# Expert weights of a two-layer mixture-of-experts kernel: one 2 MB transfer per block in place of two of 1 MB, issued once the whole buffer has been read

## What is computed

```python
def grouped_moe(x, router_w, router_bias, w_gate, w_up, w_down):
    ...                       # choose 2 of 16 experts per token: gates, [256, 16]
    def step(acc, ew):
        g_e, wg_e, wu_e, wd_e = ew          # 1024x512, 1024x512, 512x1024
        h = jax.nn.silu(x2 @ wg_e) * (x2 @ wu_e)
        return acc + (h @ wd_e) * g_e[:, None].astype(x2.dtype), None
    out, _ = lax.scan(step, jnp.zeros_like(x2), (gates.T, w_gate, w_up, w_down))
```

## Time and profile before

| | before |
|---|---|
| median of 3 runs | 1217.49 us (1212.24 to 1218.31) |
| the profiled execution: its own time | 1220.65 us |
| its span in the profile | 1218.8 us |
| mean granted TensorE clock | 0.982 of full |
| TensorE matmul busy | 1151.2 us, 94% |
| VectorE / ScalarE / GpSimd busy | 617.4 / 457.6 / 221.7 us |
| SP's hardware queue: bytes, share of 16 engines | 313.08 MB, 66.5% |
| expert transfers of 1024 KB | 192 |

### The profile page before, as it was taken

One profiled execution on the slowest core, in us unless ns is written; L12 is line 12 of the kernel. 1 busy time (PEld: TensorE's weight loads), 2 busy tenths in 40 slices (PEclk: granted clock), 3 DMA queues, 4 the chain that ended last, 5 costly groups with the idle time before them and its releaser, 6 DMA issues.

```text
span 1218.8 us, 16391 instructions
## 1 busy us (share of the span) xinstructions
PE 1151.2 (94%) x6658; PEld 809.5 (66%) x6658; DVE 617.4 (51%) x880; ACT 457.6 (38%) x712; POOL 221.7 (18%) x194
## 2 busy tenths in 40 slices
PE   7999999999979998999999898999999889999998
PEld 6967644544338876644444346889887766998997
DVE  3696612222135777612122135884599884645544
ACT  3334411211033575411211025474565534434442
POOL 5500000000010000000000000487798541000000
PEclk9999899999999999799999999999999999999999
DMA  9488799999996346899999985453343332463560
GB/s 322 131 258 326 306 380 422 422 421 421 421 384 216 139 173 239 349 372 423 421 420 421 421 323 175 157 187 106 131 178 139 138 138 69 159 255 140 182 232 35
DMA packets 86885, 321.58 MB, mean 264 GB/s; under 512 B 7160, under 2 KB 18853, under 8 KB 62235
## 3 DMA queue, kind: packets, MB, share of 16 engines
q1 hardware_dynamic: 84064, 313.08, 66.5%
q0 software_dynamic: 2192, 7.23, 1.8%
q10 hardware_dynamic: 554, 0.22, 0.1%
HBM read 318.55 MB, written 1.96 MB: 263 GB/s over the span
## 4 chain that ended last, share of the span: by engine, by line
PE 68%; DVE 15%; ACT 6%; DMA 5%; POOL 2%; issue 2%; SPq 1%; DVEq 0%; ACTq 0%
PE bank L1703 33%; PE bank L1889 15%; PE bank L1962 8%; DMA arena<-in_moe_w_down_dram 5%; DVE w_lo L712 3%; POOL w_lo L712 2%; ACT w_hi L1113 2%; PE bank L1974 2%; PE bank L1880 1%; PE bank L1785 1%; SPq L844 1%; PE bank L1922 1%; DVE arena L3145 1%; DVE rows L3126 1%; DVE arena L3163 1%
## 5 line engine op out<-in xcount | busy, mean ns | idle before, releaser
L1113 ACT ACTIVATE w_hi<-ring 128x2048 fp32r<-128x2048 f32 (+1 forms) x102 | 191.7, 1883 | 199.1 <-PE bank L1703 199.0
L712 POOL TENSOR_TENSOR w_lo<-ring,w_hi 128x512 fp32r<-128x512 f32 (+1 forms) x124 | 178.3, 1471 | 438.2 <-ACT w_hi L1113 438.2
L712 DVE TENSOR_TENSOR w_lo<-ring,w_hi 128x2048 fp32r<-128x2048 f32 x71 | 161.8, 2283 | 147.0 <-ACT w_hi L1113 146.9
L1703 PE MATMUL bank<-x_hi,w_hi 128*128 128x256 f32 x680 | 113.9, 290 | 2.8 <-issue 2.8
L1703 PE MATMUL bank<-x_hi,w_lo 128*128 128x256 f32 x680 | 110.0, 284 | 3.3 <-POOL w_lo L712 2.1
L1703 PE MATMUL bank<-x_lo,w_hi 128*128 128x256 f32 x680 | 109.7, 284 | 0.8 <-DVE x_lo L2480 0.7
L1889 PE MATMUL bank<-ring,moe_x 128*64 128x512 f32 x336 | 99.4, 595 | 4.2 <-DMA arena<-in_moe_w_up_dram 2.7
L2781 DVE TENSOR_TENSOR y_r<-bank,y_r 128x512 fp32r<-128x512 f32 x32 | 22.1, 692 | 158.1 <-ACT y_r L1113 158.1
L1703 PE MATMUL bank<-w_hi,x_hi 128*128 128x512 f32 x320 | 92.7, 404 | 7.4 <-DVE x_lo L2603 2.9
L1703 PEld LDWEIGHTS bank<-x_hi,w_hi 128*128 128x128 f32 x680 | 94.6, 193 | 6.1 <-issue 5.6
L1703 PEld LDWEIGHTS bank<-x_hi,w_lo 128*128 128x128 f32 x680 | 94.0, 192 | 3.9 <-POOL w_lo L712 2.5
(11 more groups left out here) (371 smaller groups left out, 1719.7 us busy)
## 6 DMA issues: line engine op xcount, KB each, us to landing
ring<-in_moe_w_gate_dram SPq DMA_DIRECT2D x30, 1024.0 KB, 17.1
ring<-in_w_in_dram SPq DMA_DIRECT2D x15, 2048.0 KB, 8.1
arena<-in_moe_w_up_dram SPq DMA_DIRECT2D x26, 1024.0 KB, 16.9
arena<-in_moe_w_gate_dram SPq DMA_DIRECT2D x24, 1024.0 KB, 15.5
ring<-in_moe_w_up_dram SPq DMA_DIRECT2D x24, 1024.0 KB, 18.8
arena<-in_moe_w_down_dram SPq DMA_DIRECT2D x24, 1024.0 KB, 18.8
wslots<-in_moe_w_down_dram SPq DMA_DIRECT2D x24, 1024.0 KB, 22.2
ring<-in_w_mlp_up_dram SPq DMA_DIRECT2D x8, 2048.0 KB, 8.8
```

The costliest lines, as they stand in the source:

```text
L712: last = ops.tensor_tensor(part(w_lo, label, hb)[:, x].bitcast(F32R), ring_half(label, hb)[:, x], part(w_hi, label, hb)[:, x], ALU.subtract)
L1113: return s.activation(dst, src, ACT.Copy)
L1703: last = mm(bank(use_)[0:still.shape[1], at:at + cols], still, moving, start=start and opens and (hb, n, k) == (0, 0, 0), stop=stop and cl ...
```

## The change

A block that has no half apart is issued as one transfer of 2 MB (`load`, L820 of the changed kernel). In the loop over the later blocks, SP no longer waits for `half_read`; it waits for `was_read` of the old block and then issues the new one, block after block. The three EARLY blocks still come as halves, and their first half also waits for `was_read` now. The semaphore `half_read` is still raised, and nobody waits for it.

```diff
--- before.py
+++ after.py
@@ -570,8 +570,7 @@
-            whole = label[0] in ("gate", "up", "down") and (label[0], label[2]) not in {**APART, **EARLY}
-            slot_due[slot] += 32 if whole else 16
+            slot_due[slot] += 16
@@ -875,9 +874,11 @@
                     if (kind, e) == ("up", 0):
                         load_half(("gate", l, 0), 1)
+                    if (kind, e) not in followers:
+                        load(label)
+                        continue
                     load_half(label, 0)
-                    if (kind, e) in followers:
-                        kind, e = followers[kind, e]
+                    kind, e = followers[kind, e]
                     if (kind, e) != ("down", 2):
                         load_half((kind, l, e), 1)
@@ -885,17 +886,12 @@
-                for n in range(len(slots), len(MOE_BLOCKS), 2):
-                    for hb in range(2):
-                        for kind, e in MOE_BLOCKS[n:n + 2]:
-                            if hb and (kind, e) in EARLY:
-                                continue
-                            before = blocks[kind, l, e]["before"]
-                            if hb == 0:
-                                half_read(sp, before[0])
-                            else:
-                                was_read(sp, *before)
-                            load_half((kind, l, e), hb)
+                for kind, e in MOE_BLOCKS[len(slots):]:
+                    was_read(sp, *blocks[kind, l, e]["before"])
+                    if (kind, e) in EARLY:
+                        load_half((kind, l, e), 0)
+                    else:
+                        load((kind, l, e))
```

## The result

| | before | changed |
|---|---|---|
| median of 20 runs each | 1217.35 us | 1220.28 us |
| ratio to before, 95% interval | | 1.0029 (1.0017 to 1.0040) |
| profiled execution: time, span | 1220.65, 1218.8 us | 1220.4, 1218.6 us |
| bytes from 200 to 320 us | 50.52 MB | 51.34 MB |
| up 0 to up 7, layers 0 and 1 | 188.07, 189.23 us | 188.76, 188.71 us |

A forecast was written before the change was run, and what follows sets the result against it. The DMA queue was taken to bound both expert stages, up to the last landing. Per layer 3.4 us of delay less 2.4 us from wider rows, twice, gave +2.0 us on 1217.49: 1219.5 us, range 1213 to 1227.

The forecast's parts named there:

- What bounds the kernel: Expert stages: the DMA queue at 421 GB/s bounds them; each stage's end is time of the restart + bytes / rate.
- Part 1: Queue restart in each expert stage: first halves wait for the whole product, restart 3.4 us later, two layers +6.8 us.
- Part 2: Behind each restart: rows of 16 KB in place of 8 KB give 427 GB/s, two layers -4.8 us.
- Part 3: SP's 84 fewer instructions, its new waits and the byte order within a pair: no cost or gain.
- rival C: Stage end: if the wait ahead of down 7 grew, the last product would lose 1.7 us; +5.4, 1222.9 us; chance 0.05.
- the prediction's signs: Expected in the profile: TensorE's gaps at the end keep their places, the first growing by 1 us.
- A: Full DMA stretch: rate stays at 421 GB/s and the delay is paid; +6.8, 1224.3 us; chance 0.20.
- B: Full DMA stretch: longer rows move worse, 412 GB/s, one engine holding landings up; 14.8 us slower, 1232 us; chance 0.05.
- D: DMA queue: a cost per transfer goes as 1 MB transfers are halved in number; about -10 us, 1207; chance 0.05.
- E: Full DMA stretch: rows of 16 KB save double the line's gain; -2.7 us, 1214.8; chance 0.10.
- F: Later in a stage: the queue runs dry once more; up to +3.4 us in a layer, 1220.5 to 1223; chance 0.05.

The follow-up runs named there:

- late halves: Kernel before with one wait exchanged: first halves are also issued only when the old product is done, 8 KB rows and 1 MB transfers kept; ratio 1.0055.
- three pairs early: Changed kernel with the first three pairs of the loop again in halves, the first half issued once the old half has been read; ratio 0.9978.
- six pairs early: Changed kernel with the first six pairs of the loop again in halves, the first half issued once the old half has been read; ratio 0.9955.
- the changed kernel with extra matmuls: Changed kernel with three extra matmuls of 128x512 between down 6 and up 7, their result overwritten; ratio to the kernel before 1.0009.
- the kernel before when the slow product moved onto the path: Kernel before with two extra matmuls of 128x512 ahead of down 6, their result overwritten; ratio to the kernel before 1.0002.

## Why the prediction was right

It said 1219.5 us, +2.0, with 0.26 for more than 0.5% either way; the median of after is 1220.28, the ratio +3.5 us. Two profiles of each kernel now give the ledger over both layers, from up 0 to the start of up 7 and on to down 7:

| term | predicted | shown |
|---|---|---|
| first halves late | +6.8 | 382.7 (late halves) - 377.1 (before, mean of two) = +5.6 |
| rows of 16 KB | -4.8 | 377.4 (changed, mean of two) - 382.7 = -5.3 |
| clock at the end | 0 | 24.2 - 20.8 = +3.4 |
| sum | +2.0 | +3.7, timed +3.5 |

The two terms that were worked out are right in sign and near in size, and together they are +0.3 in place of +2.0. The 3.4 us that bring the sum to +3.7 are a term that the prediction had put at nothing. That the number came out so close is in part luck.

- **What bounds the kernel** held up to the landing of up 7, in both kernels. The prediction took the end of the stage to be the landing of down 7; that held nothing up (the handover of 0.84 us is the same without it), and TensorE's own 10.41 us lie between. The step was nearly harmless for the sum, since both landings move together, but it hid that anything that lengthens up 7 counts in full.
- **Part 1, the delay.** The moves of the issues came out as worked, 3.4 us, with the dry microsecond. The effect at the far end was 3.4 us in layer 0 and 2.0 to 2.5 in layer 1. Part of that difference is there right behind the restart. In the first 30 us from up 0 on, the kernel before moved 11.35 MB in layer 0 and 11.15 in layer 1 (11.41 and 11.10 in its second profile), the kernel with late halves 10.47 and 10.60. So it was behind by 0.88 and 0.55 MB: 0.33 MB, 0.8 us, less in layer 1. The kernel before has a second dip there, right behind the window at 531:

```profile
532.00:533.00 1.00, 1.00 (x6) 0.35 (x4) 0.00 (x0) 0.00 (x0) 0.00 (x0) 1.00 0.91 123
533.00:534.00 1.00, 1.00 (x8) 0.47 (x6) 0.00 (x0) 0.00 (x0) 0.00 (x0) 1.00 0.54 172
```

Why the queue restarts less evenly in layer 1 is open.

- **Part 2, the rows.** The line through 8 KB and 1 KB rows gave 427 GB/s; 427 and 428 were measured, and 8.5 ns a packet became 9.1. The choice of the line over either bound was right. Two small slips in it changed nothing: the 37.0 ns are for 1000 bytes and not for 1 KB, with 8.4 ns for the packet; and the "about 1300" packets per 40 us should have been some 1170 by its own figures, where 1174 were counted from 212 to 252 us.
- **Part 3, what costs nothing.** SP's fewer issues and the order of bytes within a pair left no trace. That late issues cost nothing behind the dry spells is supported (at most 0.34%) and not more than that.
- **The step that was missing** is in rival C. It priced the slow product rightly at 1.7 us, and said that it "would need more than 1 us more between two landings", ahead of down 7. The loss came on up 7, one product earlier, and the gaps did not keep their places as the prediction's signs had it: in the changed kernel TensorE stood idle 1.19, 1.81 and 2.85 us in turn in layer 0, ran the products behind the first two waits at full clock and began the third at the lower one. Why the loss moved is not shown. The waits alone do not tell: before, layer 1 had 1.36, 1.95 and 1.31 us with the loss on down 6, and in the second profile 0.87, 1.95 and 3.01 with no loss at all. I had looked only at whether the last wait would grow, not at which product the loss would move to. The rival had 0.05 and was the nearest to what happened, in its sum (+5.4) worse than the forecast, in its mechanism better.
- Rivals A, B, D and E are out by the rate (they wanted 421, 412, or 433 and more); F did not occur in the changed kernel, whose share of busy engines is 1.01 over both full stretches.

## What to carry to other kernels

When a queue is the bound, an issue that comes later costs only where the queue runs dry, so look for the dry stretches first and keep the early, fine-grained issues just there; behind them take the widest rows that a transfer can have. Six of 40 blocks in early halves and the rest whole gave both advantages. And where two resources are nearly level at the end of a stage, allow for one product at the lower clock, and ask of each product whether a later landing hides it: the same 1.7 us was free on one product and on the critical path on the next. Which product it falls on could not be worked out from the waits here; a few matmuls ahead of the one that counts kept it at full clock in every profile.

## What the runs showed of the hardware

Three row lengths agree with one cost of a packet: about 9 ns on each of the 16 engines at rows of 4, 8 and 16 KB, with 409, 421 and 428 GB/s. A transfer as such cost some 7 ns of queue time or less when the queue was full. The Trainium skill (DMA: Bandwidth & Descriptors, Anatomy of one DMA) gives 2.0 us of fixed time per transfer for the other issue path; in the full queue here this was hidden, as 2 MB took 4.981 us in two transfers and 4.901 in one.

Not expected: which product meets the lower clock does not follow from the wait right before it. Up 7 ran slow after 2.85 us in the changed kernel and at full clock after 2.85 us with three pairs early and after 3.00 us with late halves (there gate 7 had run slow just before, 5.35 in place of 3.65 us, after a wait of 2.15). With six pairs early both happened in one execution, after 2.86 us in both layers. And the 3.4 us that the lower clock adds in profiles appeared in the timed ratios only in part: 0.2% came back in the changed kernel with extra matmuls, and nothing was lost in the kernel before when the slow product moved onto the path. Whether the other timed executions meet the lower clock as often is open. Their mean granted clocks do not settle it: 0.9846 in the changed kernel with extra matmuls against 0.9824 and 0.9829 without, but the kernel before alone ranges from 0.9829 to 0.9847 between sets of runs.
